# A two-layer PEER kernel: the second half of the key stage sums each slab on VectorE, and the value stage keeps five raw slabs and four row places

## The reference, cut to what matters

```python
def block(args):
    xb, ib, gb = args
    hid = jnp.einsum('td,tkd->tk', xb, u[ib])
    act = jax.nn.gelu(hid, approximate=False) * gb
    return jnp.einsum('tk,tkd->td', act, v[ib])
```

## Time and profile before

| | |
|---|---|
| three timed runs, median (lowest to highest) | 3220.83 us (3206.32 to 3223.16) |
| the profiled execution, its own time | 3211.88 us |
| its span, first to last instruction | 3210.1 us |
| mean granted TensorE clock | 0.989 of full speed |
| PE / PEld / DVE / ACT / POOL busy | 97 / 79 / 83 / 62 / 18% |
| moved by DMA | 969 MB, 302 GB/s over the span |

### The profile page before, as it was taken

How to read it: one execution, slowest core, us unless ns; L and a number is a source line. 1 busy time by engine, 2 the same in 40 slices (tenths; PEclk the granted TensorE clock), 3 DMA queues, 4 the chain that set the end, 5 groups by cost and what they waited for, 6 DMA issues and landing times.

```text
span 3210.1 us, 51808 instructions
## 1 busy us (share of the span) xinstructions
PE 3125.0 (97%) x19468; PEld 2540.1 (79%) x19468; DVE 2664.5 (83%) x3291; ACT 1980.5 (62%) x3383; POOL 592.9 (18%) x266
## 2 busy tenths in 40 slices
PE   9999999999999999999999999999999999999998
PEld 8888878998899966666668887899899986566665
DVE  5785669997899878899987757898799988889887
ACT  4444545554899955555665545555499986555556
POOL 0000000013212234433310000012322223433330
PEclk9999999999999999999999999999999999999999
DMA  7554245789999999999974344588999999999994
GB/s 270 185 194 146 94 162 186 293 334 355 367 386 390 386 381 377 375 377 393 385 266 158 115 153 152 189 320 329 356 377 384 391 374 412 373 362 378 380 380 191
DMA packets 169220, 969.08 MB, mean 302 GB/s; under 512 B 18912, under 2 KB 52704, under 8 KB 55648
## 3 DMA queue, kind: packets, MB, share of 16 engines
q1 hardware_dynamic: 132192, 698.61, 58.1%
q0 software_dynamic: 36864, 268.45, 20.7%
HBM read 951.26 MB, written 15.73 MB: 301 GB/s over the span
## 4 chain that ended last, share of the span: by engine, by line
PE 52%; DMA 8%; DVE 8%; ACT 5%; issue 2%; DVEq 0%; ACTq 0%; SPq 0%
PE ps L1112 51%; DVE halves L2010 4%; DMA raw<-in_u 3%; ACT wh L672 2%; DMA hring<-h_scratch 2%; DMA arena<-in_v,idx 2%; ACT hot_w L864 1%; DMA h_scratch<-hring 1%; DVE arena L2028 1%; DVE arena L2254 1%; DVE hot L2191 0%; PE ps L1390 0%; ACT arena L741 0%; ACT hring L849 0%; DVE arena L1943 0%
## 5 line engine op out<-in xcount | busy, mean ns | idle before, releaser
L1112 PE MATMUL ps<-xx,wh 128*128 128x384 f32 (+1 forms) x5504 | 1323.8, 360 | 7.4 <-DVE xx L1845 5.4
L1112 PEld LDWEIGHTS ps<-xx,wh 128*128 128x128 f32 x5504 | 963.4, 189 | 74.0 <-issue 7.0
L1112 PE MATMUL ps<-wh,act 128*128 128x512 f32 x3584 | 961.3, 407 | 0.1
L2010 DVE SCALAR_TENSOR_TENSOR halves<-raw,wh 128x2048 f16<-128x2048 f32 x366 | 836.3, 2287 | 114.6 <-issue 75.3
L1112 PE MATMUL ps<-halves 128*128 128x192 f16 (+2 forms) x6144 | 801.0, 295 | 46.9 <-DVE halves L2010 46.7
L1112 PEld LDWEIGHTS ps<-wh,act 128*128 128x128 f32 x3584 | 679.0, 190 | 165.3 <-issue 2.3
L1112 PEld LDWEIGHTS ps<-halves 128*128 128x128 f16 (+1 forms) x6144 | 448.6, 100 | 342.6 <-issue 249.6
L672 ACT ACTIVATE wh<-raw 128x2048 fp32r<-128x2048 f32 x366 | 698.3, 1908 | 24.8 <-DMA raw<-in_u 18.9
L1801 POOL DMA_INDIRECT arena<-in_urows,idx x128 | 221.8, 1733 | 1806.5 <-DVE idx L2146 1013.4
L1801 POOL DMA_INDIRECT arena<-in_v,idx x128 | 362.3, 2830 | 691.4 <-DVE arena L2254 667.4
L1836 DVE TENSOR_TENSOR wl<-raw,wh 128x1024 fp32r<-128x1024 f32 x240 | 292.3, 1221 | 158.4 <-ACT wh L658 157.4
(11 more groups left out here) (241 smaller groups left out, 2043.5 us busy)
## 6 DMA issues: line engine op xcount, KB each, us to landing
raw<-in_u SPq DMA_DIRECT2D x256, 1024.0 KB, 7.4
raw_far<-in_v SPq DMA_DIRECT2D x142, 1024.0 KB, 8.1
raw<-in_w SPq DMA_DIRECT2D x118, 1024.0 KB, 4.9
raw<-in_v SPq DMA_DIRECT2D x114, 1024.0 KB, 8.2
h_scratch<-hring SPq DMA_DIRECT2D x128, 96.0 KB, 7.1
hring<-h_scratch SPq DMA_DIRECT2D x128, 96.0 KB, 7.5
arena<-in_memT SPq DMA_DIRECT2D x4, 512.0 KB, 7.2
raw<-in_w SPq DMA_DIRECT2D x4, 512.0 KB, 7.7
```

Source lines behind the costliest of these rows:

```text
L1112: return nc.tensor.matmul(out, lhs, rhs, start=start, stop=stop, **kw)
L2010: v.scalar_tensor_tensor(out=wl16[:, j:j + 2, :], in0=raw_slab(p // 2).rearrange("p (e c) -> p e c", e=2), scalar=W_UP, in1=wh[:, j:j + 2, ...
```

## The change

1. In the key stage, from slab 64 on, `take_side` and `fold` are left out. VectorE adds the two halves of the PSUM bank in one `tensor_reduce` into `hring` (a new function, `summed`), and ScalarE's Gelu works in place in `hring`. `summed(k)` stands on VectorE right behind `low_slab` of slab k+2; those of the last two slabs stand behind the loop. The wait for the store that frees the place of `hring` moves from Gelu to `summed`.
2. FAR goes from 4 to 2, so the value stage has five raw places instead of seven. The space goes to two more row places: value gathers (all but the first two of a layer) rotate through four places, those of the keys through the two of before (`gather_places`).
3. LOAD_LAG goes from 3 to 1: the load of a stored Gelu stands one slab behind the value slabs on SyncE's queue.

```diff
-FAR, FAR_FROM = 4, 6
+FAR, FAR_FROM = 2, 6
...
-STORE_LAG, LOAD_LAG = 4, 3
+STORE_LAG, LOAD_LAG = 4, 1
...
+def gather_places():
+
+    places, last, uses = [], {}, collections.Counter()
+    for n in range(4 * PAIRS):
+        j = n % (2 * PAIRS) - PAIRS
+        slot = (j - SLOTS) % (2 * SLOTS) if j >= SLOTS else n % SLOTS + SLOTS
+        uses[slot] += 1
+        places.append((slot, uses[slot], last.get(slot)))
+        last[slot] = n
+    return places
...
             def gelu(k, j):
                 j %= 2
-                act.wait_ge(fold_done, k + (folded(t0) + 1))
-                kept = k < KEPT
-                if not kept:
-                    stores = layer * ((S_EXP - KEPT) // HOUT) + (k - KEPT) // HOUT
-                    if stores:
-
-                        act.wait_ge(h_stored[j], 16 * stores)
-                nc.scalar.activation(h_kept[:, k, :] if kept else hring[:, j, :], ps[:, j, 0:ND],
-                                     ACT.Gelu, scale=W_DOWN).then_inc(evac_done, 1)
+                if k < KEPT:
+                    act.wait_ge(fold_done, k + (folded(t0) + 1))
+                    out, total = h_kept[:, k, :], ps[:, j, 0:ND]
+                else:
+                    act.wait_ge(halves_summed, layer * (S_EXP - KEPT) + k - KEPT + 1)
+                    out = total = hring[:, j, :]
+                nc.scalar.activation(out, total, ACT.Gelu, scale=W_DOWN).then_inc(evac_done, 1)
...
-                    take_side(u0, i * slabs + (s - 1), (s - 1) % 2, ND)
+                    if i * slabs + s <= KEPT:
+                        take_side(u0, i * slabs + (s - 1), (s - 1) % 2, ND)
...
-                           side_of=i * slabs + (folded(t0) + s - 1), x_from=RING * layer if first and s == 0 else None,
+                           side_of=None if spreads and (i > SPREAD0 or s) else i * slabs + (folded(t0) + s - 1),
+                           x_from=RING * layer if first and s == 0 else None,
...
-            if n >= SLOTS:
-                pool.wait_ge(slot_free, n - (SLOTS - 1))
-            pool.indirect_dma_start(out=gbuf[n % SLOTS], out_offset=None, in_=rows_of,
+            slot, _, held = GATHER_PLACES[n]
+            if slot < SLOTS and j < 2 * SLOTS:
+                pool.wait_ge(piece_used, (P_V0, P_V1)[n // (2 * PAIRS)] + 4)
+            elif held is not None:
+                pool.wait_ge(slot_free, held + 1)
+            pool.indirect_dma_start(out=rows_at[slot], out_offset=None, in_=rows_of,
...
+            def summed(k):
+
+                j = k % HOUT
+                stores = layer * ((S_EXP - KEPT) // HOUT) + (k - KEPT) // HOUT
+                dve.wait_ge(piece_used, u0 + 2 * k + 2)
+                if stores:
+                    dve.wait_ge(h_stored[j], 16 * stores)
+                v.tensor_reduce(hring[:, j, :], ps[:, j, 0:2 * ND].rearrange("p (a t) -> p t a", a=2), AX.X, ALU.add)\
+                    .then_inc(halves_summed, 1)
+
             for i in range(SPREAD_END - SPREAD0):
                 for n in range(WIDE):
                     q = i * Q_TRIP + COMPARE_SLAB.index(n) if n in COMPARE_SLAB else None
                     if q is not None:
                         compare(q)
                     low_slab()
+                    if i * WIDE + n >= 2:
+                        summed(KEPT + i * WIDE + n - 2)
                     if q is not None and q >= 3:
                         gate_kept(q - 3)
                     if n in DOT_SLABS:
                         dot()
...
+            summed(S_EXP - 2)
+            summed(S_EXP - 1)
```

More of the change, by code:

```diff
@@ L185, in folded @@
 def folded(slab):
-    return slab - T_WQ0 - (S_INB if slab >= T_WQ1 else 0)
+    return slab - T_WQ0 - (S_INB + S_EXP - KEPT if slab >= T_WQ1 else 0)
 def half_of(p):
@@ L226 @@
 RAW_PLACES = raw_places()
+def gather_places():
[7 more added lines that the diff above has]
+    return places
+GATHER_PLACES = gather_places()
 def rope_chunk(n):
@@ L431, in build @@
     x_free = x_space[:, :, 0:NS]
+    rows_far = nc.alloc_sbuf_tensor_at("rows_far", [P, SLOTS, D], F32, offset=xx_at + FAR * 2 * PC * 4)
+    rows_at = [rows_far[:, j, :] for j in range(SLOTS)] + gbuf
     raw_far = nc.alloc_sbuf_tensor_at("raw_far", [P, FAR, 2 * PC], F32, offset=xx_at)
@@ L488, in build @@
     sidx_ready, rep_ready, idx_ready = sem("sidx_ready"), sem("rep_ready"), sem("idx_ready")
-    gath_in = [sem(f"gath_in{j}") for j in range(SLOTS)]
+    gath_in = [sem(f"gath_in{j}") for j in range(2 * SLOTS)]
     slot_free, vacc_ready = sem("slot_free"), sem("vacc_ready")
@@ L494, in build @@
     up_ready, vacc_up = sem("up_ready"), sem("vacc_up")
+    halves_summed = sem("halves_summed")
     act_own, dve_own, dve_settled = sem("act_own"), sem("dve_own"), sem("dve_settled")
@@ L909, in experts @@
                 trip(i, WIDE, spread=True, spread_first=i == SPREAD0)
-            take_side(u0, S_EXP - 1, 1, ND)
             gelu(S_EXP - 1, S_EXP - 1)
@@ L1540, in experts @@
                 trip(i, WIDE, spreads=True)
-            fold(folded(t0) + S_EXP - 1, 1, NS)
             pe.wait_ge(gs_ready, layer + 1)
@@ L1798, in gather @@
         def gather(rows_of, n, j):
-            if n >= SLOTS:
-                pool.wait_ge(slot_free, n - (SLOTS - 1))
-            pool.indirect_dma_start(out=gbuf[n % SLOTS], out_offset=None, in_=rows_of,
+            slot, _, held = GATHER_PLACES[n]
[4 more added lines that the diff above has]
+            pool.indirect_dma_start(out=rows_at[slot], out_offset=None, in_=rows_of,
                                     in_offset=bass.IndirectOffsetOnAxis(ap=idx[:, j:j + 1], axis=0))\
-                .then_inc(gath_in[n % SLOTS], 16)
+                .then_inc(gath_in[slot], 16)
         for layer in range(2):
@@ L2018, in gathered @@
             def gathered(n):
-                dve.wait_ge(gath_in[n % SLOTS], 16 * (n // SLOTS + 1))
-                return gbuf[n % SLOTS]
+                slot, use, _ = GATHER_PLACES[n]
+                dve.wait_ge(gath_in[slot], 16 * use)
+                return rows_at[slot]
             def dot():
@@ L2141, in experts @@
                         if layer:
-                            dve.wait_ge(gath_in[(2 * PAIRS - 1) % SLOTS], 16 * ((2 * PAIRS - 1) // SLOTS + 1))
+                            slot, use, _ = GATHER_PLACES[2 * PAIRS - 1]
+                            dve.wait_ge(gath_in[slot], 16 * use)
                         own.mark(v.tensor_scalar(idx[0:NS, :], ps[0:NS, 7, 0:PAIRS], float(layer * KEYS * KEYS), None,
```

## The result

The changed kernel takes 3483.78 us (median of four runs, 3476.03 to 3490.68) beside 3219.56 for the kernel before, a ratio of 1.083 with a 95% interval of 1.079 to 1.087: slower by 264 us. The forecast was 3500 (3440 to 3580). The span of its profiled execution is 3482.3 us, 272.2 above that of before. In the experiments one execution fell out, one of four of the run with the writes ahead of Gelu, at 14013 us: its ratio leaves it out, its median of 3275.84 us counts it (the other three have 3274.35).

The account below looks back on a forecast made before the run. TensorE was taken to set the pace, with VectorE and ScalarE close behind. Wide trips +293, hand-over +6 and value stages -15 gave +284 us on 3211.9, or 3496; on the median 3505, forecast 3500, range 3440 to 3580.

Parts of the forecast that it names:

- reduce of 384 to 192: VectorE's new PSUM reduce per slab: 0.55 us, taken between rows of neighbouring sizes, with 0.42 and 0.69 as ends.
- a slab with gate copy and writes: Wide trips: 5.07 us for a bare slab, plus 0.27 for the gate copy and 2.42 for the eight writes.
- wide stretch of 62 slabs: Key stage of each layer: 441 us after the change, at 7.15 us per slab against 4.65 before.
- added there, both layers: Wide trips of both layers: 145 + 148 = 293 us more.
- hand-over to the value stage: Key stage's end: last slab's reduce waits for slab 125's store, gates' last copies behind it; 3 us per layer, 6 in all.
- both value stages: Four row places remove most waits behind late gathers: -15 us, between -30 and 0.
- The circle: Wide trips: high part, low part, reduce and Gelu wait in turn across ScalarE and VectorE, 7.15 us per slab; chance 0.83.
- What is hidden: Wide trips: TensorE's saved 0.17 us per slab worth nothing; VectorE's other work costs nothing where ScalarE has writes.
- VectorE's idle time in the kernel before: Wide trips before: 0.36 us per slab, read as VectorE waiting for TensorE to be done with slab m-2.
- The low clock: Rival: idle time keeps TensorE at 1.2 GHz in the wide trips, 9.0 us per slab, 3760 us; chance 0.04.
- covered by 3 us: Wide trips: a single TensorE slab at low clock, up to 9 us, fits some 12 us and costs nothing.
- VectorE's sum of work: Rival: Gelu's wait hidden, VectorE sets the wide trips' pace at 4.77 us per slab, 3220 us; chance 0.05.

Follow-up runs that it names:

- the run with the writes ahead of Gelu: Changed kernel with one exchange on ScalarE: gate copy and eight writes stand ahead of Gelu; 3275.84 us, ratio 1.0189 to the kernel before.
- The exchange on VectorE: Changed kernel with the reduce of slab m-2 put first, ahead of the low part of slab m; 3252.64 us, ratio 1.0117 to the kernel before.
- the value part alone: Kernel before with FAR 2, four row places and LOAD_LAG 1 only; 3185.15 us, ratio 0.9913; repeated at 3185.35 and 3189.33 us.
- the run with five raw places: Kernel before with FAR 2 and LOAD_LAG 1 but still two row places; 3210.03 us, ratio 0.9999.
- the runs with the order mended: Changed kernel with the reduce ahead of the low part, 3252.64 us; the same with the reduce ahead of compare too, 3236.59 us.
- the run with positions 2, 4 and 7: Value part plus VectorE summing only these three of eight wide-trip slabs, reduce ahead of compare; 3193.93 us, ratio 0.9926 to the kernel before.
- the last run: The run with positions 2, 4 and 7, but slab 127 keeps side copy and identity product; 3183.80 us, ratio 0.9906 to the kernel before.

## Why the prediction was right, step by step

| step | forecast | measured | from |
|---|---|---|---|
| reduce of 384 to 192 | 0.55 us | 0.550 | L2223 |
| a slab with gate copy and writes | 5.07 + 0.27 + 2.42 = 7.76 | 7.70 | 1002.83 to 1010.53 |
| wide stretch of 62 slabs | 441 and 441 us | 445.7 and 444.1 | the writes' rows |
| added there, both layers | +293 | +300 | less 296.2 and 293.4 |
| hand-over to the value stage | +6 | -1 | last group of writes to first value product |
| both value stages | -15 (-30 to 0) | -25 | first value product to the norm behind the stage |
| sum on the span | +284 | +272 | 3482.3 - 3210.1 |

*The circle* holds as it was put: one slab is the sum of high part, low part, reduce, Gelu and what stands between Gelu and the next high part. The exchange on VectorE broke it, down to waits in two slabs of eight, and the exchange on ScalarE shortened it to near the length worked out. Gelu waits for the reduce 124 times, 366.8 us in all, 2.96 each, where 2.9 in each of 126 slabs was forecast.

*What is hidden* was read rightly too: TensorE's 0.17 us per slab gained nothing, VectorE's dot, compare and gate product cost nothing beside the writes. The slab without writes whose VectorE work is longer shows in the timeline as well (5.82 us against 5.32 for the other one, the 0.5 us that were forecast): there the high part starts at 1011.07, but VectorE goes from the dot (1010.75) over a compare to its low part at 1013.56.

*The hand-over* was mis-sized. I put 6 us for the store that frees the last slab's place. With the transfer engines at two thirds of their load a store lands in 2.1 us in the median, where it took 7.1 before, so there was next to nothing to wait for. In the run with the reduce first, whose wide trips again move 346 GB/s, the two hand-overs come to 28.5 us against 22.1 in the changed kernel and 23.2 before, which fits; that it is the whole reason was not tested.

*The value stages* gave 25 us where I took 15, inside the bounds. The rows of the value part alone show the cause that I gave, gathers asked for too late, and the run with five raw places that they cost nothing.

*The sum* is closer than its terms: the circle cost 7 us more than forecast, the hand-over 7 less and the value stages gave 10 more, so the misses cancel in part. That is luck, though each of them is small beside the 293 us of the circle.

*One reading was wrong.* VectorE's idle time in the kernel before was put down to TensorE being at work on slab m-2. The trace says otherwise:

```profile
1018.70 1.90 ACT L672 ACTIVATE wh<-raw 128x2048 fp32r<-128x2048 f32 x1
...
1020.69 2.29 DVE L2010 SCALAR_TENSOR_TENSOR halves<-raw,wh 128x2048 f16<-128x2048 f32 x1 [1.53 <-issue]
```

The low part starts 0.09 us after ScalarE's high part ends, and so does every other one between 900 and 1100 us with idle time of 0.2 us and more ahead of it. TensorE had ended slab m-2 some 3 us earlier. The sum uses the idle time nowhere, so it isn't hurt. But VectorE hung on ScalarE's high part before the change too, and this is the tie that holds it up in the runs with the order mended.

*The low clock* came, as the rival had it, and did not decide. In the wide windows the granted clock lay between 0.83 and 0.94, and the slabs took the same time at either level, as shown above. Two high passes of TensorE in the changed kernel's trace:

```profile
1238.75 4.57 PE L1128 MATMUL ps<-xx,wh 128*128 128x384 f32 x16 [2.87 <-ACT hring L866]
...
1244.56 3.08 PE L1128 MATMUL ps<-xx,wh 128*128 128x384 f32 x16
```

The first, after 2.87 us of idle time, took 4.57 us instead of 3.05; the granted clock from its start at 1238.70 to 1242.10 is 0.50. But there is no idle time ahead of the second: the slow pass used up the gap that it would have had anyway. It was covered, as I had put it with "covered by 3 us". The Trainium skill (TensorE: Matmul & The Clock Gate, "HAM oscillation — how this bites in real kernels") tells that a wait between bursts of products makes every next burst start at the low clock. This trace agrees in part: 4.57 us after 2.87 us of idle time, but 3.05 us after 2.85.

Where TensorE is what the others wait for, the low clock does cost time, and the forecast has no term for it at the hand-over. The first 12 value products of the two stages take 5.23 and 4.51 us in the changed kernel and 2.96 each with the value part alone. That is 3.8 us, which is the whole difference between their value stages (1093.7 and 1089.9 us).

*VectorE's sum of work*, the rival at 3220, is not what the changed kernel ran into. It is a good part of what is left once the circle is broken: a slab has 4.77 us of VectorE's work, and takes 5.2 and 5.1 us in the runs with 3253 and 3237.

What stays open: in the run with positions 2, 4 and 7 the value stages, whose code is that of the value part alone, take 1095.1 us against 1089.9. The low clock in their first products accounts for 4.5 of the 5 us (5.20 and 5.26 us against 2.96 each). Everything but the wide trips, the hand-overs and the value stages takes 1480.2 us against 1472.5, 1475.7 and 1478.3 in the three traces of the value part alone; for that I have no cause, and it may be no more than how traces differ. And whether the last run gains anything over the value part alone would need more runs.

## What to carry to other kernels

Sums of work per engine give a bound, not the pace. Before a dependency goes to another engine, write down for one round what stands ahead of the new producer and behind the new consumer in their queues; if the consumer's own predecessor feeds the producer's predecessor, the two engines take turns, and the round costs the sum of all of it. Then do the same over two rounds: a looser circle can be left. When such a circle is found, exchange neighbours in the queues before anything is taken back: here two lines were worth 231 us.

A load whose consumer waits is not a sign that the transfer engines are full: here two more places for gathers raised them from 377 to about 400 GB/s, and two places fewer for the raw slabs cost nothing.

## What the runs showed of the hardware

- The same idle time is followed by either clock. After 2.85 us of idle time the high pass at 1010.95 ran at a granted clock of 1.00 (3.05 us for 16 products); after 2.87 us the one at 1238.75 began at 0.50 and took 4.57 us.
- A lower TensorE clock alone cost nothing where another engine set the pace: a slab of 7.48 us at a mean granted clock of 0.66, of 7.47 us at 1.00.
- A second reduce of 0.55 us per slab on VectorE, which was busy for 91% of the stretch without it, made a slab 0.33 us longer (42 us in 128), while VectorE's idle time before its low part fell from 0.43 to 0.26 us per slab.
- The transfer engines moved 401 GB/s over 278 us with up to four gathers and five slabs asked for, where the same two stretches of the kernel before show 377 and 379 GB/s. A gather of 1 MB took 11.0 to 11.5 us from issue to landing in both.
